# Key scaling moved to ScalarE, another order of the weight parts, and a new last step and ending for a fused mixer and mixture-of-experts layer

## The reference, cut to what matters

```
lb = cumsum(softmax(hgrn_lb_logits)); lb = lb - lb[:1]
mod = silu(c) @ w_ada + b_ada                        # six shift/scale/gate vectors
h = rmsnorm(x, norm1_g) * (1 + scale1) + shift1
z = h @ w_in                                          # q, v, zf, zb, og, u, gz
log_f = logaddexp(log(lb), log1p(-lb) + log_sigmoid(z));  k = (1 - lb) * sigmoid(-z)
...                                                   # scan in two directions, convolution, gates, w_out
x1 = x + gate1 * mix
h = rmsnorm(x1, norm2_g) * (1 + scale2) + shift2
scores, top-8 of 64 experts;  routed = sum_e combine * (silu(g) * u) @ down_e;  shared expert
x2 = x1 + gate2 * (routed + shared)
y = rmsnorm(x2, final_norm_g)
```

## Time and profile before

| | us |
|---|---|
| median of 3 runs | 872.17 (870.12 to 873.66) |
| the profiled execution's own time | 869.49 |
| its span, first to last instruction | 867.4 |
| busy in the span: PE, DVE, ACT, POOL | 810.0, 387.8, 226.6, 68.9 |
| mean granted TensorE clock | 0.981 of full speed |

### The profile page before, as it was taken

How to read it: one execution, slowest core, us unless ns; L and a number is a source line. 1 busy time by engine, 2 the same in 40 slices (tenths; PEclk the granted TensorE clock), 3 DMA queues, 4 the chain that set the end, 5 groups by cost and what they waited for, 6 DMA issues and landing times.

```text
span 867.4 us, 13089 instructions
## 1 busy us (share of the span) xinstructions
PE 810.0 (93%) x5330; PEld 555.7 (64%) x5330; DVE 387.8 (45%) x788; ACT 226.6 (26%) x365; POOL 68.9 (8%) x54
## 2 busy tenths in 40 slices
PE   4999999999999989989999999699999999899973
PEld 2688989899999979964545455254554745354221
DVE  1148899779988656573232312122221121122104
ACT  2254435334435244231111111011121111012002
POOL 1000737600000010100000000000000000000000
PEclk9999999999999999999999999899999999999988
DMA  8997878342342639978999999999999999999993
GB/s 322 387 386 278 286 273 291 131 158 99 120 173 98 203 122 368 393 291 346 364 415 418 417 418 416 415 418 420 414 417 410 416 416 419 415 419 418 416 409 133
DMA packets 81206, 284.71 MB, mean 328 GB/s; under 512 B 5240, under 2 KB 12024, under 8 KB 64504
## 3 DMA queue, kind: packets, MB, share of 16 engines
q1 hardware_dynamic: 80648, 282.55, 83.7%
q10 hardware_dynamic: 496, 1.30, 0.4%
HBM read 280.67 MB, written 3.16 MB: 327 GB/s over the span
## 4 chain that ended last, share of the span: by engine, by line
PE 65%; SPq 18%; DMA 9%; DVE 3%; POOL 3%; issue 2%; ACT 1%; DVEq 0%; POOLq 0%
SPq L616 16%; PE bank L2096 11%; PE bank L2152 6%; PE bank L1686 6%; PE bank L1691 6%; PE bank L1688 6%; DMA chunk<-in_w_expert_down 5%; PE bank L1672 3%; PE bank L1980 3%; PE bank L1748 3%; PE bank L2003 3%; PE bank L1633 3%; DMA chunk<-in_w_expert_gate_up 2%; PE bank L1708 2%; PE bank L1710 2%
## 5 line engine op out<-in xcount | busy, mean ns | idle before, releaser
L2096 PE MATMUL bank<-chunk,xg 128*64 128x512 f32 (+2 forms) x1024 | 201.7, 622 | 19.8 <-DMA chunk<-in_w_expert_gate_up 19.6
L2096 PEld LDWEIGHTS bank<-chunk,xg 128*64 128x64 f32 (+2 forms) x1024 | 62.8, 131 | 152.3 <-issue 136.3
L2152 PE MATMUL bank<-chunk,act_t 128*64 128x512 f32 (+2 forms) x512 | 101.0, 611 | 3.7 <-DMA chunk<-in_w_expert_down 3.7
L1496 DVE SCALAR_TENSOR_TENSOR act_r<-bank,w_slot,sil 128x256 f32<-128x256 f32 x26 | 12.6, 483 | 181.9 <-ACT sil L977 181.9
L1508 DVE TENSOR_TENSOR y_lo<-bank,y_hi 128x512 fp32r<-128x512 f32 x52 | 36.0, 692 | 73.9 <-ACT y_hi L990 73.9
L977 ACT ACTIVATE sil<-bank 128x256 f32<-128x256 f32 x26 | 10.0, 385 | 210.6 <-PE bank L2096 210.6
L2152 PEld LDWEIGHTS bank<-chunk,act_t 128*64 128x64 f32 (+2 forms) x512 | 31.1, 128 | 52.2 <-issue 51.3
L1065 DVE TENSOR_TENSOR ring_lo<-ring,ring_hi 128x1024 fp32r<-128x1024 f32 x44 | 52.6, 1219 | 18.8 <-ACT ring_hi L769 18.5
L670 POOL TENSOR_TENSOR small<-small 128x4 f32<-128x4 f32 (+2 forms) x9 | 9.2, 1027 | 651.9 <-DVE small L1578 486.1
L990 ACT ACTIVATE y_hi<-bank 128x512 fp32r<-128x512 f32 x52 | 31.1, 597 | 102.2 <-PE bank L2152 102.2
L1125 DVE SCALAR_TENSOR_TENSOR conv<-upad,dw,conv 128x256 f32<-128x256 f32 x120 | 54.6, 525 | 0.0
(11 more groups left out here) (319 smaller groups left out, 1291.2 us busy)
## 6 DMA issues: line engine op xcount, KB each, us to landing
chunk<-in_w_expert_gate_up SPq DMA_DIRECT2D x128, 1024.0 KB, 21.0
chunk<-in_w_expert_down SPq DMA_DIRECT2D x64, 1024.0 KB, 22.8
ring<-in_w_in SPq DMA_DIRECT2D x16, 2048.0 KB, 10.3
ring<-in_w_ada SPq DMA_DIRECT2D x12, 2048.0 KB, 15.1
ring<-in_w_proj_hgrn SPq DMA_DIRECT2D x2, 2048.0 KB, 7.7
ring<-in_w_out SPq DMA_DIRECT2D x2, 2048.0 KB, 13.4
ring<-in_w_proj_conv SPq DMA_DIRECT2D x1, 2048.0 KB, 8.1
chunk<-in_w_shared_gate_up SPq DMA_DIRECT2D x2, 1024.0 KB, 22.8
```

Of the source, the lines that this page charges most:

```text
L2096: ins = mm(bank[2 + b][row:row + width, :], xg[:, k, c:c + width], w[:, k % 4, :], start=(k == 0), stop=(k == KD - 1))
L2152: ins = mm(out[row:row + width, :], act_t[:, c, row:row + width], w[:, c, h * 512:(h + 1) * 512], start=(c == 0), stop=(c == 1))
```

## The change

- ACT, and no longer POOL, makes the 32 scalings, four behind each pair of `split_hi` quarters of a zf or zb half.
- The first two quarters of q0's high part are made before the wait for `mod_ready` and before the first sigmoid of u2; the other two behind both sigmoids. DVE makes v0's last two low quarters two taps earlier.
- The last down chunk is loaded in two halves of 512 KB (c = 0 and c = 1), the second with a semaphore of its own; `last_down` does the 14 matmuls that don't need the second half, then the last two.
- The last scatter of step 25 waits for each half of the result and follows it with no `loop_done`; the four x1 transposes stand behind it, each into its own bank; DVE adds x1 from PSUM, so ACT's copies go. The squares are taken in halves.
- SP issues g2row before x1_back.
- Each engine's ending stands twice, under `If(n < 1)` and at the end of its `Else`; n is loaded before the last down step. The extra items scatter in their own order, with tiles of their own (not run here).

```diff
-            pool.wait_ge(vec_copied, 3)
             for half in range(2):
-                for d in range(2):
-                    for j in range(2):
-                        evacuated(pool, f"{('zf', 'zb')[d]}{half}", j)
-                        ...
-                            nc.gpsimd.tensor_scalar(fg[:, d, c], fg[:, d, c], oml[:, i:i + 1], lb[:, i:i + 1], ALU.mult, ALU.add).then_inc(fk_done, 1)
-                            nc.gpsimd.tensor_scalar(qk[:, 2 + d, c], qk[:, 2 + d, c], oml[:, i:i + 1], None, ALU.mult).then_inc(fk_done, 1)
                 pool.wait_ge(fk_done, 16 + 17 * half)
@@ ACT
             copy_partial(ada_after["u1"])
+            filled(act, "u2", 0)
+            split_hi(1, (0, 1))
             act.wait_ge(mod_ready, ada_after["u1"] + 1)
             for j in range(2):
                 filled(act, "u2", j)
                 nc.scalar.activation(tmp[:, j, :], fill_bank("u2", j)[:, :], ACT.Sigmoid).then_inc(act_evac, 1)
-                split_hi(1, (2 * j, 2 * j + 1))
+            split_hi(1, (2, 3))
@@ ACT, in the loop over zf and zb, behind split_hi
+                        act.wait_ge(vec_copied, 3)
+                        evacuated(act, f"{z}{half}", j)
+                        for hh in range(2):
+                            ...
+                            nc.scalar.activation(fg[:, d, c], fg[:, d, c], ACT.Identity, scale=oml[:, i:i + 1], bias=lb[:, i:i + 1]).then_inc(fk_done, 1)
+                            nc.scalar.activation(qk[:, 2 + d, c], qk[:, 2 + d, c], ACT.Copy, scale=oml[:, i:i + 1]).then_inc(fk_done, 1)
@@ DVE
                 if w == CW - 4:
                     split_lo(apart, (0, 1))
-            split_lo(apart, (2, 3))
+                if w == CW - 3:
+                    split_lo(apart, (2, 3))
@@ SP
-                        load_ranked(place_of(number), part, experts[item])
+                        if number < len(CHUNK_NO) - 1:
+                            load_ranked(place_of(number), part, experts[item])
+                            continue
+                        for c, loaded_half in enumerate((s_chunk[place_of(number)], s_last_half)):
+                            src = dn_src[bass.ds(experts[item], 1)][:, :, c:c + 1, :].rearrange("a p c d -> (a p) c d")
+                            sp.dma_start(dn_tile(place_of(number))[:, c:c + 1, :], src).then_inc(loaded_half, 16)
...
-            sp.dma_start(x1_back[:, :, :].rearrange("p k t -> p (k t)"), A["x1"]).then_inc(s_x1_back, 16)
             for s in range(NS):
                 sp.dma_start(g2row[:, s, :]...).then_inc(s_g2_back, 16)
+            sp.dma_start(x1_back[:, :, :].rearrange("p k t -> p (k t)"), A["x1"]).then_inc(s_x1_back, 16)
@@ PE
+            def last_down():
+                ...
+                def one(h, c, item):
+                    row, width = SLOTS_OF[n][item]
+                    return mm(bank[2 + h][row:row + width, :], act_t[:, c, row:row + width], tiles[item][:, c, h * 512:(h + 1) * 512], start=(c == 0), stop=(c == 1))
+                for h in range(2):
+                    for c in range(2):
+                        for item in range(items - c):
+                            one(h, c, item)
+                pe.wait_ge(s_last_half, 16)
+                for h in range(2):
+                    one(h, 1, items - 1).then_inc(dn_done, 1)
...
             n_extra = pe.value_load(nwork, min_val=0, max_val=NX)
-            ...
-            pe.wait_ge(loop_done, 1)
-            x1_to_tokens(0)
-            x1_to_tokens(1)
-            for s in range(NS):
-                for h in range(2):
-                    ins = scatter(1, s, h, last=True)
-                ins.then_inc(y_done, 1)
-            x1_to_tokens(2)
-            x1_to_tokens(3)
+            last_down()
+            def finish():
+                for h in range(2):
+                    pe.wait_ge(y_ready, 2 * NSTEPS - 1 + h)
+                    for s in range(NS):
+                        scatter(1, s, h, last=True).then_inc(y_done, 1)
+                pe.wait_ge(s_x1_back, 16)
+                for j in range(4):
+                    x1_to_tokens(j)
+            with pe.If(n_extra < 1):
+                finish()
+            with pe.Else():
+                ...
+                finish()
@@ DVE, the ending
             def gated_y(s):
-                dve.wait_ge(y_done, s + 1)
                 for hf in range(2):
+                    dve.wait_ge(y_done, 3 + s)
             def residual(s):
-                dve.wait_ge(x1_copied, 2 * s + 2)
-                V.tensor_tensor(fin[:, s, :], fin[:, s, :], x1[:, s, :], ALU.add).then_inc(x2_done, 1)
+                for hf in range(2):
+                    dve.wait_ge(x1_ready, 2 * s + hf + 1)
+                    V.tensor_tensor(fin[:, s, c], fin[:, s, c], bank[2 * s + hf][:, :], ALU.add).then_inc(x2_done, 1)
```

More of the change, by code:

```diff
@@ L208, in build @@
         y_hi = [at(f"y_hi{i}", 197 + 2 * i, [P, 512], F32R) for i in range(2)]
+        y_hi_x = [at(f"y_hi_x{i}", 48 + 2 * i, [P, 512], F32R) for i in range(2)]
+        y_lo_x = [at(f"y_lo_x{i}", 52 + 2 * i, [P, 512], F32R) for i in range(2)]
+        sel_t_x = at("sel_t_x", 0, [P, T], F32R)
         y_lo = [at(f"y_lo{i}", 176 + 2 * i, [P, 512], F32R) for i in range(2)]
@@ L499, in build, with extras @@
         iota_x = consts_x[0:NE, X_IOTA:X_IOTA + NX]
-        def extras(eng, first, pair):
-            eng.wait_ge(items_done, 2)
-            n = eng.value_load(nwork, min_val=0, max_val=NX)
-            with eng.If(n > 0):
+        def extras(eng, n, first, pair, finish):
+            with eng.If(n < 1):
+                finish()
+            with eng.Else():
                 first()
@@ L2154, in down_halves @@
                     ins.then_inc(dn_done, 1)
+            def last_down():
+                n, items = NSTEPS - 1, ITEMS_OF[NSTEPS - 1]
+                for item in range(items):
+                    chunk_loaded(pe, n, 2, item)
+                pe.wait_ge(t_evac, n + 1)
+                tiles = [dn_tile(place_of(CHUNK_NO[n, 2, item])) for item in range(items)]
+                def one(h, c, item):
[8 more added lines that the diff above has]
+                    one(h, 1, items - 1).then_inc(dn_done, 1)
             def down(n):
@@ L2186, in _, with x1_to_tokens, finish @@
                     gather_next(i, weights_of(n + 1))
-                down(n)
+                if n < NSTEPS - 1:
+                    down(n)
             n_extra = pe.value_load(nwork, min_val=0, max_val=NX)
-            with pe.If(n_extra > 0):
+            last_down()
+            def x1_to_tokens(j):
+                s, hf = j // 2, j % 2
+                for i in range(4):
+                    ins = nc.tensor.transpose(bank[j][:, i * P:(i + 1) * P], x1_back[:, 4 * hf + i, s * P:(s + 1) * P], ident)
+                ins.then_inc(x1_ready, 1)
+            def finish():
+                for h in range(2):
+                    pe.wait_ge(y_ready, 2 * NSTEPS - 1 + h)
+                    for s in range(NS):
+                        scatter(1, s, h, last=True).then_inc(y_done, 1)
[3 more added lines that the diff above has]
+            with pe.If(n_extra < 1):
+                finish()
+            with pe.Else():
                 gather_next(NIT - 1, extra_weights(0))
@@ L2202, in _ @@
-                        act_to_channels(1, i * 2 + 1)
-                        with pe.If(n_extra > i * 4 + (4 - 4 * NIT)):
-                            gather_next(i, extra_weights(0))
-                        extra_down(1, i)
-            def x1_to_tokens(j):
-                s, hf = j // 2, j % 2
-                pe.wait_ge(x1_copied, j - 1) if j >= 2 else pe.wait_ge(s_x1_back, 16)
-                for i in range(4):
-                    ins = nc.tensor.transpose(bank[j % 2][:, i * P:(i + 1) * P], x1_back[:, 4 * hf + i, s * P:(s + 1) * P], ident)
-                ins.then_inc(x1_ready, 1)
@@ L2215, in _ @@
-            pe.wait_ge(loop_done, 1)
-            x1_to_tokens(0)
-            x1_to_tokens(1)
-            for s in range(NS):
-                for h in range(2):
-                    ins = scatter(1, s, h, last=True)
-                ins.then_inc(y_done, 1)
-            x1_to_tokens(2)
-            x1_to_tokens(3)
+                        for b in range(2):
+                            pe.wait_ge(y_ready, i * 4 + (2 * b - 1))
+                            pe.wait_ge(y_ready, i * 4 + 2 * b)
+                            extra_gate_up(b, i)
+                            act_to_channels(b, i * 2 + b)
+                            if b == 0:
+                                second_turn(i, extra_weights(1))
+                            else:
+                                with pe.If(n_extra > i * 4 + (4 - 4 * NIT)):
+                                    gather_next(i, extra_weights(0))
+                            extra_down(b, i)
+                            for h in range(2):
+                                pe.wait_ge(y_ready, i * 4 + (2 * b + h + 1))
+                                for s in range(NS):
```

(2 more changed lines are left out.)

90 lines of the change are left out of this document (44 added, 46 removed).

## The result

| | before | after |
|---|---|---|
| median of the runs, us | 871.17 (870.12 to 873.66, 4 runs) | 861.12 (861.04 to 862.36, 4 runs) |
| the profiled execution, us | 869.49 | 862.36 |
| its span, us | 867.4 | 860.5 |
| busy: PE, DVE, ACT, POOL, us | 810.0, 387.8, 226.6, 68.9 | 809.0, 385.1, 238.9, 20.0 |
| mean granted TensorE clock | 0.981 | 0.982 |

The changed kernel is faster: a ratio of 0.9884 with an interval of 0.9858 to 0.9909. The direction was right, the size too small by 5.4 us. These 10.05 us between the medians are the largest difference of the study: two repetitions, further down, gave 8.4 and 7.9.

A forecast was written before the change was run, and what follows sets the result against it. PE bounds the projections, the chunk stream the expert loop, then a chain behind the last chunk. Projections 3.3 plus last step and ending 2.4 make 5.7 us: 863.8 from the profiled execution, 866.5 as median, range 863.6 to 870.2.

The forecast's parts named there:

- The step that failed: Whole kernel: carried the 2.7 us between the profiled execution and the runs' median over, turning 863.8 into 866.5 us.
- Projections, 3.3: First 166 us: three PE gaps (1.13, 1.21, 0.58 us) go, plus about 0.4 of matmul overlap; bounds 2.9 and 3.5.
- the 1.21 us at v0: PE's gap ahead of v0's third quarter: goes because 8 taps move behind the low quarters, which come 3.2 us earlier.
- the 8 taps of 0.67 us each: DVE in the projections: 8 taps took 5.39 us beside POOL's scalings, while 12 without them took 4.83.
- The size of the scalings: ACT in zf and zb: 0.3 to 0.41 us each, four making 1.2 to 1.6 us, covered by a 2.78 us pause.
- Last step: Last down matmuls: PE starts about 845.9, 1.1 us earlier; last two calls 0.9 us apart, so the split alone brings 0.2.
- Ending, 2.4: From the last step to the end: 2.4 us shorter, gate2 times y starting 2.55 us earlier; bounds 0.5 and 3.5.
- Doubling the ending costs nothing: Ending in both arms: 0 us on the path, n tested during waits and the second copy's jump behind the last work.
- The first (3.3 come back): Later chain or chunk stream takes back the projections' 3.3 us: 869.8 us, chance 0.15.
- The second: A jump into the ending takes all of PE's 2.47 us pause, 1.3 us staying on the path: 867.8 us, chance 0.11.
- The third: x1_back, issued behind g2row, lands 8.0 us after PE wants it: 874.5 us, chance 0.06.
- The fourth: More than forecast: last calls run densely (0.9 us) and DVE leaves no other gap: 865.0 to 864 us, chance 0.11.

The follow-up runs named there:

- proj_only: Kernel before with only the projection edits (scalings on ACT, q0's and v0's quarters earlier): median 867.05 us, ratio 0.9953 to the kernel before.
- whole_chunk: Changed kernel with the usual order of the last 16 calls and both chunk halves awaited first: 863.52 us, ratio 0.9904 to the kernel before.
- doubled_only: Kernel before with only the ending of PE, ACT and DVE written in both arms of the condition: 868.86 us, ratio 0.9988 to the kernel before.
- end_only: Kernel before with only the changes of the last step and the ending: 866.15 us, ratio 0.9944 to the kernel before.
- orders_only: Kernel before with only q0's high and v0's low quarters reordered, scalings left on POOL: 870.03 us, ratio 0.9992 to the kernel before.
- act_only: Kernel before with only the 32 scalings moved from POOL to ACT: 868.62 us, ratio 0.9974 to the kernel before.
- wait_at_need: Changed kernel with the last 16 calls in usual order, the second chunk half awaited where first needed: 861.97 us, ratio 0.9895 to the kernel before.
- x1_through_sbuf: Changed kernel with ACT copying x1 to SBUF and DVE adding it from there: 862.06 us, ratio 0.9893 to the kernel before.
- one_ending: Changed kernel with each engine's ending written once, behind the condition, so engines jump over the extra items: 865.60 us, ratio 0.9936 to the kernel before.
- busy_wait: Kernel before with 14 unread matmuls added between the last down matmul and the jump: 873.64 us, ratio 1.0032 to the kernel before.
- before_look_2: Kernel before, unchanged, profiled a third time: 871.94 us in one run.
- before_look_1: Kernel before, unchanged, profiled a second time: 869.16 us in one run.

## Why the prediction was right or wrong

The 5.35 us between 866.47 and 861.12 have three parts:

- **1.0**: the median of the first three runs, 872.17, stood that far above the median with the fourth (871.17).
- **2.9**: in medians the kernels stand 10.05 us apart, their profiled executions only 7.13 (that of before lies 1.68 under its median, that of after 1.24 over).
- **1.4**: the profiled executions stand 7.13 apart where my sum had 5.7.

*The step that failed* is therefore first of all this one: "the median of the runs is 2.7 us above that execution, and from its 872.17 it is 866.5". It takes the distance between one execution and the median for a constant that the changed kernel inherits, and 3.9 of the 5.35 us are on it. It is no constant: it was 1.68 us below the median for before and 1.24 above it for after. Much of it goes with stretches at half clock, which some executions have and others don't. The profiled one of before had none in its ending and lay at the fast end (869.49 in 868.6 to 874.5); that of after had one in its gather and lay at the slow end of its first four. A part of it is luck. The two repetitions stand 8.4 and 7.9 us apart where the first measurement had 10.05, so some 2 us of the miss belong to that one set of four and four runs, and 2.2 to 2.7 us of it are left against my 5.7. The spans of the three traces of each kernel are 7.4 us apart in the mean (868.1 and 860.7).

The change may also take away one of the places of half clock. Of six traces with the old ending two are at half clock in the transposes and the scatter (9.83, 9.85 for 8.24 to 8.32), of eight with the new one and no jump none is. A third and a fourth (proj_only, 9.35, and whole_chunk, 7.47) are so in the down matmuls, behind a wait of 3.08 and 2.81 us for the chunk, a place that both endings have. PE idles for 2.3 to 2.8 us in the old ending and 1.4 in the new. That the shorter pause is why the clock holds is argued from these few traces and not tested. The 12 runs of doubled_only (868.02 to 872.36), with 1.84 us, are spread only a little less than those of the kernel before; the 8 of end_only (865.37 to 866.80) much less.

*Projections, 3.3: right in kind, 0.4 too small.* The scores come 3.70 us earlier (3.75 by the count above); the half clock in the gather hides 0.7 of it in that one trace. I overlooked a fourth gap, 0.33 us ahead of v0 with no releaser but "issue", which went too. The working had two wrong links. I gave the 1.21 us at v0 to DVE's order alone; orders_only shows that it goes by the order, and act_only that it goes without it, once POOL's scalings are gone. With the orders alone it comes back as a wait for k_sum. And the 8 taps of 0.67 us each that I put beside POOL's scalings stood beside its sum of the keys (113.78 to 116.58): the same 8 take 5.40 us in act_only, which has the sum and no scalings. Beside the scalings 12 taps took 5.64 to 5.94 us for 4.83, a tenth of a microsecond each at most. The size of the scalings was under what was measured (0.50 and 0.60, not 0.30 to 0.41), without consequence, because the row of 128x256 taken as nearest was of another function (a sigmoid) and the pause was wide enough.

*Last step: right in this trace.* PE starts where I put it (842.51 for 842.6), 1.4 us earlier than before in end_only. The other two traces of the changed kernel have 844.37 and 841.34, so the 0.1 us is luck. That the last two calls would stand 0.9 us apart was wrong: all 16 took 3.67 us as before. But they came at the same point for the first half, and the first product with gate2 stood at 849.34 for 849.4. What I missed is that the old order could be kept and be better (wait_at_need).

*Ending, 2.4: mis-sized, 3.8 in the trace of end_only.* The part from the down matmuls to gate2 is exact (6.83 for 6.8). The rest, 1.4 us, was missing: 0.3 by the earlier start, 0.2 to the mean (the squares never showed), 0.4 between mean and last product, in which stands POOL's inverse root, which took 1.48 us before, beside DVE's sum of two SBUF tensors, and 0.55 after, beside DVE's sum from PSUM (0.94 in x1_through_sbuf), and 0.5 behind the last final product (4.0 for 4.5). That last one is neither the doubling (4.5 in doubled_only) nor its absence (3.9 in one_ending), nor x1's way (3.9). It lies in the last store. In all eight traces with the old ending an instruction block of 8 KB (queue q14) comes 2.0 us before the end, in the middle of that store, and the store's last six packets of 2 KB then end one after another, 0.08 us apart, up to 0.5 us behind all the others. None of the nine with the new ending has a block there, and all their packets end together. The view of before (865.2 to 866 us) has it, that of after (857.9 to 860) has not:

```profile
q1 hardware_dynamic: 154, 0.26, 89.4%
q14 instruction: 1, 0.01, 2.4%
```

```profile
q1 hardware_dynamic: 288, 0.52, 66.8%
```

That the block holds up the packets behind it is read from these 17 traces and not tested; why it is fetched just then in the old ending alone is open.

*"Doubling the ending costs nothing", "this trace shows no stall of its own": wrong about the trace, harmless to the sum.* The 2.47 us were the jump. They lay beside 1.9 us of other work, and my sum took them away without saying so, since it let the scatter follow the low part at once. Without this edit the new ending would have brought little: from the down matmuls to the end of the span before takes 20.4 us, the doubling alone makes 19.8, the rest without it 22.1 (with PE at half clock, and a start of the down matmuls that is the second earliest of all), both 18.0. In time, the interval of one_ending (0.9922 to 0.9950) overlaps with that of proj_only (0.9937 to 0.9969), which has nothing of the new ending.

*The rivals.* The first (3.3 come back) is false: in proj_only the last down matmuls began 3.3 us earlier, and its median is 4.2 us lower. The second had the mechanism and the size right (2.44 us) but the wrong sign of its effect: it was paid before and not after. The third is false: x1_back landed 9.4 us after its issue, at about 849.3, though the margin is nearly used up. The fourth had the sign, and too little of it.

## What to carry to other kernels

When a kernel's runs spread over 0.6%, profile it two or three times before you add a trace's difference to a median: its stretches at half clock can put that execution 1 or 2 us off, and the medians of one set of runs can lie 2 us off as well (10.05, then 8.4 and 7.9 here). A jump over code that is not run cost PE 2.4 us or more in this kernel: it was free only beside other work, and shortening that work brought little until the path that is taken was the one that falls through. Before crediting an order for a gap, ask which engine slowed the one that was late, and look at what that engine was running at that very time.

## What was not expected of the hardware

- A jump over a loop: 2.44 us of PE with nothing to wait for (busy_wait), 3.72 in one_ending, and 16 KB on an instruction queue in that time. In the second the block starts 1.26 us after PE's last matmul, in the first 0.29 us before it ends.
- An 8 KB instruction block in the middle of the last store: some of its packets end up to 0.5 us late (eight traces of eight with it, none of nine without).
- PE fell from 2.4 to 1.2 GHz (granted 0.50) after it had idled in the ending for 3.72 us (one_ending), 2.83 (orders_only), 2.78 (before_look_2) and 2.44 (busy_wait), ahead of the last down matmuls after waits of 3.08 (proj_only) and 2.81 (whole_chunk), and not after 2.58 (before_look_1), 2.56 (act_only), 2.50, 2.30 (proj_only), 1.84 and 1.41. Pauses of about 2.5 us went both ways, and in the first gather it fell with no pause of over 1 us ahead of it.
- POOL's 128x1 root took 1.48 us beside a DVE sum of two SBUF tensors 1024 wide, 0.94 beside such a sum in halves and 0.55 beside one with an operand in PSUM. DVE's 120 taps took 54.6 us beside POOL's scalings and 50.6 without (act_only).
- ACT scaling 128x256 from SBUF by a value for each partition: 0.50 us (Copy), 0.60 us (Identity with bias).
- x1_back needed 9.4 us from issue to landing behind the two g2row transfers, where it had needed 19.9 ahead of them: a later issue is not a landing later by as much. That fewer chunks were under way by then is argued, not tested.
